# Hybrid pooling and DeltaNet layer: sample's output rows in plain fp32 from refetched raw weights in four column groups, the last z product ahead on VectorE, sample's input rows behind the gate

## The chip, the cores and the metric

The kernel runs on one core of one Trainium2 chip. The metric is the device time of one execution in microseconds; the median over several runs counts. TensorE (PE) multiplies, VectorE (DVE), ScalarE (ACT) and GpSimd (POOL) do elementwise work, and SyncE (SP) issues every DMA from one queue, in program order. PE takes its instructions in program order too, so a wait in front of one instruction holds all behind it.

## What is computed

One decoder layer runs over a prompt of 2048 tokens and over a "sample" of 8 tokens with carried state. The part that the change touches is the output projection of the 8 sample tokens, the products of the SiLU gate, and the input rows of the sample.

```python
h = rms_norm(x, pre_norm_w) * (1.0 + scale[:, None]) + shift[:, None]
proj = h @ w_in                       # u_a, z_a, q, k, v, z_b, b, a
y_a, new_pool = pool_mix(u_a, ...)    # pooling mixer, 4 groups
y_a = y_a * jax.nn.silu(z_a)
o, S = gdn_chunked(q, k, v, g, beta, S0)      # prompt
o, S = gdn_recurrent(q, k, v, g, beta, S0)    # sample: one step per token
o = rms_norm(o, o_norm_w) * silu(z_b)
y = concatenate([y_a, y_b], -1) @ w_out       # [tokens, 1024] @ [1024, 1024]
x = x + gate[:, None] * rms_norm(y, post_norm_w)
```

All of it is in fp32, inputs and outputs.

## The kernel before

The prompt is cut into four blocks of 512 tokens (`it` 0 to 3; the last is `LAST`). Every block runs through 32 weight tiles (`NW`): 0 to 11 are q, k and v, 12 to 23 are z and u, 24 to 31 (`OUT` + m) are quarters of the output projection. Each fp32 weight is split into two rounded parts, hi and lo, and each activation too, so that one fp32 product becomes three fp32r matmuls: hi with hi, hi with lo, lo with hi. Block 0 splits the weights (ScalarE the hi, GpSimd the lo) and SP keeps the pair in DRAM (`kept_w`, 1 MB a tile); the later blocks load the pair into a ring of three slots `wsl`, three tiles ahead: the load of tile n waits until tile n - 3 has been used (`proj`).

`out_tile(it, m)` (L2170 to L2172) does 24 matmuls of 512 columns. Its m from 0 to 3 makes output columns 0 to 511 (`hf` 0), m from 4 to 7 the rest (`hf` 1). The first reads of an accumulator bank wait for VectorE's product of z tile 23, `zmul` (L1370), which frees that bank. Between the tiles of phase two runs a plan of 27 slots with the DeltaNet chain; m = 0 falls in slot 24, m = 1 in slot 26.

In the last block the sample rides along. For the output projection `sample_out(it, m)` (L2236 to L2238) takes the 8 rows `ym2`, split into hi and lo, through the same split weight tile that `out_tile(it, m)` uses: six matmuls with 8 stationary columns and 512 moving ones for each of the eight m, which collect in one bank for each half (`so` 0 and 1). VectorE copies the half to `ys` (`sample_half`, L1401). `sample_state(it, m)` (L2289) multiplies the key rows `krow` (VectorE, L1548), which the new states `ssm` need (L1559, L1563). At the very end `ys` is squared (ScalarE), its root taken (GpSimd), then scaled and added on VectorE (L1849, L1852), before VectorE weighs the last prompt rows (`weigh_rows`, L1286) and adds them to the residual (L1864).

SP's function `load_tile` loads the kept tiles, `xres` brings the residual rows of the prompt (L817), and behind the last of these come sample's inputs and the outputs.

Of the kernel before, what the change touches and what calls it, by code (L numbers as in the profile page):

```python
# [20 lines left out]
F32 = mybir.dt.float32  # L21
# [143 lines left out]
def psum_jobs(it):  # L165
# [25 lines left out]
    for slot, (c, p, sc, q, parts) in enumerate(PLAN):  # L191
# [64 lines left out]
def sample_plan_steps():  # L256
# [4 lines left out]
             "pool": [f"pl{i}" for i in range(9)], "mixed": ["ym0", "ym1", "ym2", "yma", "yh", "yl"],  # L261
# [22 lines left out]
def sample_out_steps():  # L284

    out = []
    for m in range(8):
        out += ["krow0", "krow1"] if m == 0 else [f"krow{m + 1}"] if m < 7 else []
        out += ["ys0"] if m == 4 else []
# [6 lines left out]
    "pe": ["hs"] + [f"{kind}{n}" for kind, n in JOBS[-1] if kind in SAMPLE_JOBS and kind != "so"],  # L296
    "act": ["x_sq"] + sample_act_steps() + ["y_sq"],
    "pool": ["rx0", "rx", "clear", "half", "rk", "rstd", "ry0", "ry"],
    "dve": (["xn", "h0", "h", "hh", "hl"] + ["g_a", "pg0", "g_beta", "g_sp", "g_g", "pg1", "g_d0", "g_d1"] + sample_plan_steps() + sample_out_steps() + ["ys1", "yn", "yr"]),
# [3 lines left out]
def layer_kernel(nc, a):  # L303
    ctx = ExitStack()
    with ctx:
# [83 lines left out]
        lb = over("lb", rp, 0, [P, BS, BS])  # L389
        epar = sb("epar", [P, 2])  # L390
# [10 lines left out]
        ym2 = sb("ym2", [P, 8, 2 * NS], F32R)  # L401
# [286 lines left out]
        def _(sp):  # L688
# [40 lines left out]
            def load_tile(it, t):  # L729
# [3 lines left out]
                if it == LAST and t - WS >= OUT:  # L733
                    sp.wait_ge(*done("pe", f"sp{t - WS}"))
# [4 lines left out]
                sp.dma_start(slot_words(n), kept[t]).then_inc(w_in[n % WS], 16)  # L739

# [22 lines left out]
            def block_of(it, last=False):  # L763
# [8 lines left out]
                for t in range(NW):  # L772
# [377 lines left out]
        def _(dve):  # L1150
# [247 lines left out]
            def sample_half(it, hf):  # L1398

                dve.wait_ge(*done("pe", f"sp{OUT + 4 * hf + 3}"))  # L1400
                nc.vector.tensor_copy(ys[:, hf * BT:(hf + 1) * BT], bank("so", hf)[0:NS, :]).then_inc(*step("dve", f"ys{hf}"))  # L1401

            def sample_slot(it, slot):
# [123 lines left out]
                if slot == SAMPLE_SLOT["mixed"]:  # L1527
# [6 lines left out]
                    after("yma")  # L1534
                    after("ymb")
                    nc.vector.tensor_copy(ym2[:, :, 0:NS], ym[:]).then_inc(*s("yh"))
                    after("yh")
                    nc.vector.tensor_tensor(ym2[:, :, NS:], ym[:], ym2[:, :, 0:NS].bitcast(F32), ALU.subtract).then_inc(*s("yl"))

            def sample_out(it, m):  # L1540
# [54 lines left out]
            def block_of(it, last=False):  # L1595
# [3 lines left out]
                for t in range(NQ):  # L1599
# [25 lines left out]
                    if t == GATES + 2 and it == 0:  # L1625
                        sample_rows()
# [13 lines left out]
                    if t == GATES + 2:  # L1640
# [9 lines left out]
                                                ALU.mult).then_inc(g_g.sem, 1)  # L1650
                    for c in GB_AT.get(t, ()):
# [45 lines left out]
                for slot, (c, p, sc, q, parts) in enumerate(PLAN):  # L1697
# [147 lines left out]
                if last:  # L1845
                    sample_half(it, 1)
# [187 lines left out]
        def _(pe):  # L2034
# [189 lines left out]
            def sample_out(it, m):  # L2224

                hf, kp = divmod(m, 4)
                t = OUT + m
                pe.wait_ge(*weights_in(it, t))
                pe.wait_ge(*done("dve", "yl"))
                if kp == 0:  # L2230
                    bank_free(pe, it, "so", hf)
                for j in range(2):
                    k = 2 * kp + j
# [304 lines left out]
```

## Time and profile before

| | before |
|---|---|
| median of 3 runs | 1060.54 us (1058.96 to 1061.08) |
| profiled execution | 1061.8 us, of which the span from the first to the last instruction is 1060.0 us |
| PE busy | 1019.4 us, 96% of the span |
| VectorE, ScalarE, GpSimd busy | 642.8, 391.2, 218.6 us |
| mean granted TensorE clock | 0.989 |
| HBM read, written | 156.43 MB, 44.81 MB |

Lines "L12" are lines of the kernel before. A row of a timeline gives the start, the duration, the engine, the line and what is written from what; matmuls are pipelined, so a matmul of 512 columns shows some 0.39 us but the next one starts 0.23 us later. In brackets stands how long the engine was idle before, and what ended that. A plain fp32 matmul leaves two records (x2 for one). PEclk is the granted clock, 1.00 for 2.4 GHz and 0.50 for 1.2 GHz.

### The profile page before, as it was taken

Reading aid. Unit: us, or ns where it says so; the run is one execution under the profiler, and the core shown is the slowest. Engines: PE = TensorE matmul, PEld = TensorE weight load, DVE = VectorE, ACT = ScalarE, POOL = GpSimd, SP = SyncE. Lnnn points to the kernel's source line nnn. Section 1 sums busy time; section 2 is a strip of 40 time slices with the busy share of each in tenths; the row PEclk is TensorE's granted clock in tenths of the full one; section 3 lists DMA queues with packets and bytes.
Section 4 is the critical chain, followed back from the end, with each engine's and each line's share of the span. In section 5 each row is a group of like instructions: output and inputs, shape, how many; then the busy total and the mean of one; then the engine's idle time right before and its main releaser. Section 6 shows DMA issues by size and latency. Waiting matters only on the chain.

```text
span 1060.0 us, 16762 instructions
## 1 busy us (share of the span) xinstructions
PE 1019.4 (96%) x6235; PEld 796.3 (75%) x6235; DVE 642.8 (61%) x1344; ACT 391.2 (37%) x773; POOL 218.6 (21%) x222
## 2 busy tenths in 40 slices
PE   4999999999999999999999999999999999999995
PEld 1577677877777788887877788887877788888774
DVE  2468896577355784576356874576255765555644
ACT  4277532433725621323435621414426631121211
POOL 0143545555400102221000102230000100533000
PEclk9999999999999999999999999999999999999998
DMA  8597665373867553244656553254674343322265
GB/s 333 221 354 257 238 252 233 120 257 131 307 214 274 188 190 142 97 160 146 253 200 235 199 198 119 82 192 149 255 293 159 120 159 120 116 77 88 89 241 177
DMA packets 46804, 202.33 MB, mean 191 GB/s; under 512 B 9162, under 2 KB 9930, under 8 KB 29188
## 3 DMA queue, kind: packets, MB, share of 16 engines
q1 hardware_dynamic: 46724, 201.26, 52.0%
q8 instruction: 50, 0.82, 0.3%
q14 instruction: 30, 0.25, 0.1%
HBM read 156.43 MB, written 44.81 MB: 190 GB/s over the span
## 4 chain that ended last, share of the span: by engine, by line
PE 80%; DVE 6%; issue 4%; DMA 3%; ACT 2%; POOL 2%; SPq 1%; DVEq 0%; ACTq 0%; POOLq 0%
PE acc L2133 15%; PE acc L2135 14%; PE acc L2134 14%; PE ring L2183 11%; PE ring L2170 2%; PE acc L2170 2%; PE ring L2171 2%; PE ring L2172 2%; PE acc L2172 2%; PE acc L2171 2%; DMA wraw<-in_w 2%; PE ring L2200 2%; PE ring L2370 1%; DVE cacc L1254 1%; PE ring L2192 1%
## 5 line engine op out<-in xcount | busy, mean ns | idle before, releaser
L2133 PE MATMUL acc<-hhi,wsl 128*128 128x512 f32 x768 | 317.7, 414 | 2.7 <-DVE y L1370 2.6
L2135 PE MATMUL acc<-hhi,wsl 128*128 128x512 f32 x768 | 301.2, 392 | 0.0
L2134 PE MATMUL acc<-hlo,wsl 128*128 128x512 f32 x768 | 300.8, 392 | 0.0
L2133 PEld LDWEIGHTS acc<-hhi,wsl 128*128 128x128 f32 x768 | 145.4, 189 | 41.4 <-issue 10.2
L2135 PEld LDWEIGHTS acc<-hhi,wsl 128*128 128x128 f32 x768 | 144.7, 188 | 31.8
L2134 PEld LDWEIGHTS acc<-hlo,wsl 128*128 128x128 f32 x768 | 145.5, 189 | 27.6 <-issue 2.2
L1254 DVE SCALAR_TENSOR_TENSOR cacc<-raw,cw,cacc 128x512 f32<-128x512 f32 x144 | 113.1, 785 | 66.3 <-ACT cacc L938 59.8
L1905 POOL TENSOR_TENSOR wsl<-wraw,wsl 128x512 fp32r<-128x512 f32 x60 | 84.9, 1429 | 104.2 <-ACT wsl L901 104.2
L934 ACT ACTIVATE raw<-acc 128x512 f32<-128x512 f32 x48 | 28.6, 596 | 123.8 <-PE acc L2135 119.3
L2170 PE MATMUL acc<-wsl,yhi 128*128 128x512 f32 x128 | 51.7, 404 | 5.2 <-DVE y L1370 3.4
L901 ACT ACTIVATE wsl<-wraw 128x512 fp32r<-128x512 f32 x64 | 38.1, 622 | 40.2 <-DMA wraw<-in_w 37.9
L1970 POOL TENSOR_TENSOR on<-on,mhalf 128x4 f32<-128x4 f32 x16 | 23.1, 1446 | 138.8 <-DVE on L1789 138.8
L2170 PE MATMUL ring<-wsl,yhi 128*128 128x512 f32 x128 | 51.1, 400 | 0.4
L2172 PE MATMUL ring<-wsl,yhi 128*128 128x512 f32 x128 | 50.4, 394 | 0.0
L2171 PE MATMUL ring<-wsl,ylo 128*128 128x512 f32 x128 | 50.3, 393 | 0.0
L2172 PE MATMUL acc<-wsl,yhi 128*128 128x512 f32 x128 | 50.0, 391 | 0.0
L2171 PE MATMUL acc<-wsl,ylo 128*128 128x512 f32 x128 | 50.0, 390 | 0.0
L1095 ACT ACTIVATE junk<-ao 128x128 bf16<-128x128 f32 x64 | 19.9, 310 | 74.5 <-DVE ao L1777 72.9
L946 ACT ACTIVATE tmpa<-acc 128x512 f32<-128x512 f32 x32 | 19.1, 597 | 69.5 <-PE acc L2135 69.1
L997 ACT ACTIVATE cq<-cacc 128x512 f32<-128x512 f32 x48 | 30.2, 629 | 31.0 <-DVE cacc L1254 30.8
L1339 DVE TENSOR_TENSOR xt<-xt,stmp 128x126 f32<-128x126 f32 (+22 forms) x124 | 37.7, 304 | 4.3
L1336 DVE TENSOR_TENSOR stmp<-lb,xt 128x126 f32<-128x126 f32 (+22 forms) x124 | 36.6, 295 | 3.6
(323 smaller groups left out, 1668.0 us busy)
## 6 DMA issues: line engine op xcount, KB each, us to landing
wsl<-kept_w SPq DMA_DIRECT2D x96, 1024.0 KB, 4.8
kept_w<-wsl SPq DMA_DIRECT2D x32, 1024.0 KB, 6.4
wraw<-in_w SPq DMA_DIRECT2D x64, 256.0 KB, 4.3
xb<-in_x SPq DMA_DIRECT2D x16, 512.0 KB, 5.7
wada<-in_w_ada SPq DMA_DIRECT2D x8, 1024.0 KB, 11.5
xres<-in_x SPq DMA_DIRECT2D x16, 512.0 KB, 5.7
out_y<-ytok SPq DMA_DIRECT2D x16, 512.0 KB, 8.0
xtr<-in_xt SPq DMA_DIRECT2D x12, 512.0 KB, 6.6
```

The costliest lines, as they stand in the source:

```text
L901: nc.scalar.activation(wsl[:, t % WS, 0, e * (KT // 2):(e + 1) * (KT // 2)], wraw[:, n % WR], ACT.Copy).then_inc(w_hi, 1)
L1254: nc.vector.scalar_tensor_tensor(out=cacc[:, t % 2], in0=r[:, j:j + BT], scalar=cw[:, t, j:j + 1], in1=cacc[:, t % 2], op0=ALU.mult, op1=A ...
L1336: nc.vector.tensor_tensor(t, lb[:, m, 0:m].unsqueeze(2).to_broadcast([P, m, n]), xt[:, m, m // 2:].unsqueeze(1).to_broadcast([P, m, n]), A ...
L1339: nc.vector.tensor_tensor(xt[:, 0:m, m // 2:], xt[:, 0:m, m // 2:], t, ALU.subtract).then_inc(sub_f.sem, 1)
L1905: nc.gpsimd.tensor_tensor(wsl[:, t % WS, 1, ks], wraw[:, n % WR], wsl[:, t % WS, 0, ks].bitcast(F32), ALU.subtract).then_inc(w_lo, 1)
L2133: nc.tensor.matmul(acc[t % 2][:], w[:, 0, k], hi[:, k], start=(k == 0), stop=False)
L2134: nc.tensor.matmul(acc[t % 2][:], w[:, 0, k], lo[:, k], start=False, stop=False)
L2135: last = nc.tensor.matmul(acc[t % 2][:], w[:, 1, k], hi[:, k], start=False, stop=(k == KT - 1))
L2170: nc.tensor.matmul(o, yhi[:, k, cols], w_hi_k, start=(k == 0), stop=False)
L2171: nc.tensor.matmul(o, ylo[:, k, cols], w_hi_k, start=False, stop=False)
L2172: last = nc.tensor.matmul(o, yhi[:, k, cols], w_lo_k, start=False, stop=(k == KT - 1))
L2183: last = nc.tensor.matmul(bank(kind, i)[rows, h * n:(h + 1) * n], left(h), right(h), start=True, stop=True)
```

## The change

Sample's output rows are made from raw fp32 weights instead of the split ones. `sample_out(it, hf)` is called twice: half 0 where m = 0 and 1 stood, half 1 in front of `sample_state(it, 5)`. Each call is eight plain fp32 matmuls with `ym` as stationary operand, k going round four column groups of 32, so four partial sums land in partitions 0, 32, 64 and 96 of one bank. VectorE adds them up (one copy and three adds for each half). The raw weights, 512 KB for each m, are fetched a second time by SP into four buffers `wout0` to `wout3` laid over other tiles. Beside it, `zmul` of tile 23 goes to the front of slot 23's work in all four blocks, and in block 0 `sample_rows` (the sample's input rows) goes behind the gate's softplus chain. The split of `ym` (two small VectorE operations) goes, and so do SP's waits for the sample's matmuls ahead of the last five weight tiles.

```diff
@@ SP
             def load_tile(it, t):
                 n = it * NW + t
                 sp.wait_ge(*proj(*divmod(n - WS, NW)))
-                if it == LAST and t - WS >= OUT:
-                    sp.wait_ge(*done("pe", f"sp{t - WS}"))
...
+            def sample_out_weights(m):
+                sp.dma_start(wout[m % 4][:].rearrange("p j c -> p (j c)"), a["w"][OUT + m].rearrange("p k c -> p (k c)")
+                             ).then_inc(raw_in[WR - 1], 16)
...   (in the loop over t, behind load_tile(it, t + WS) and xres)
+                    if last and t == OUT - 2:
+                        sp.wait_ge(*conv(it, NQ - 1))
+                        sp.wait_ge(*hist_out(it, NQ - 1))
+                        sample_out_weights(0)
+                        sp.wait_ge(*pooled_f(it, NG - 1))
+                        sp.wait_ge(*u_out(it, NG - 1))
+                        sample_out_weights(1)
+                        sample_out_weights(2)
+                    if last and t == OUT - 1:
+                        sp.wait_ge(*done("pe", f"sc{OUT // 4 - 1}"))
+                        sample_out_weights(3)
+                    if last and t == OUT + 4:
+                        sp.wait_ge(*done("pe", "so0"))
+                        for m in range(4, 8):
+                            sample_out_weights(m)
@@ DVE, sample_half
-                dve.wait_ge(*done("pe", f"sp{OUT + 4 * hf + 3}"))
-                nc.vector.tensor_copy(ys[:, hf * BT:(hf + 1) * BT], bank("so", hf)[0:NS, :]).then_inc(*step("dve", f"ys{hf}"))
+                cols = slice(hf * BT, (hf + 1) * BT)
+                dve.wait_ge(*done("pe", f"so{hf}"))
+                nc.vector.tensor_copy(ys[:, cols], bank("so", hf)[0:NS, :]).then_inc(*step("dve", f"ys{hf}a"))
+                for g, so_far, to in ((1, "a", "b"), (2, "b", "c"), (3, "c", "")):
+                    dve.wait_ge(*done("dve", f"ys{hf}{so_far}"))
+                    nc.vector.tensor_tensor(ys[:, cols], ys[:, cols], bank("so", hf)[g * BS:g * BS + NS, :], ALU.add
+                                            ).then_inc(*step("dve", f"ys{hf}{to}"))
...   (the second half: was behind the loop over m, now at m == 7, ahead of L1559)
@@ DVE, slots
             def gated(it, t):
-                zmul(it, t)
+                if t < OUT - 1:
+                    zmul(it, t)
...   (slot 23, ahead of its job "ot")
+                    if slot == LAST_PART:
+                        zmul(it, OUT - 1)
@@ PE, sample_out(it, hf) in place of sample_out(it, m)
-                for j in range(2):
-                    k = 2 * kp + j
...
-                    nc.tensor.matmul(o, ym2[:, k, 0:NS], w_hi_k, start=(k == 0), stop=False)
-                    nc.tensor.matmul(o, ym2[:, k, NS:], w_hi_k, start=False, stop=False)
-                    last = nc.tensor.matmul(o, ym2[:, k, 0:NS], w_lo_k, start=False, stop=(k == KT - 1))
+                bank_free(pe, it, "so", hf)
+                pe.wait_ge(*done("dve", "yma"))
+                pe.wait_ge(raw_in[WR - 1], 16 * (len(range(WR - 1, 2 * NW, WR)) + 4 * (hf + 1)))
+                for k in range(KT):
+                    kp, j = divmod(k, 2)
+                    g = k % NBK
+                    last = nc.tensor.matmul(bank("so", hf)[g * BS:g * BS + NS, :], ym[:, k], wout[kp][:, j], start=(k < NBK),
+                                            stop=(k >= KT - NBK))
...   (behind slot 26, the loop over m)
                 for m in range(8):
-                    if last and m >= 2:
-                        sample_out(it, m)
+                    if last and m == 5:
+                        sample_out(it, 1)
```

Three places show what moves. On PE, in the last block at m = 5 (`wsl` and `yhi` are the prompt's weights and rows, `wout` the raw weights, `ym` the sample's rows), before:

```order
L2171 MATMUL ring5<-wsl_68,ylo_53 128x512
L2172 MATMUL ring5<-wsl_68,yhi_52 128x512
L2236 MATMUL ring3<-wsl_68,ym2 8x512 [waits sample_dve,w_in1]
L2237 MATMUL ring3<-wsl_68,ym2 8x512
L2238 MATMUL ring3<-wsl_68,ym2 8x512
L2236 MATMUL ring3<-wsl_68,ym2 8x512
L2237 MATMUL ring3<-wsl_68,ym2 8x512
L2238 MATMUL ring3<-wsl_68,ym2 8x512
L2289 MATMUL ring1<-drow_114,krow_117 128x128 [waits sample_dve]
```

and of the change at the same place:

```order
L2191 MATMUL ring5<-wsl_68,ylo_53 128x512
L2192 MATMUL ring5<-wsl_68,yhi_52 128x512
L2252 MATMUL ring3<-wout0_86,ym_110 8x512 [waits raw_in2,sample_dve,ya_f]
L2252 MATMUL ring3<-wout0_86,ym_110 8x512
L2252 MATMUL ring3<-wout1_87,ym_110 8x512 x2
L2252 MATMUL ring3<-wout2_88,ym_110 8x512 x2
L2252 MATMUL ring3<-wout3_89,ym_110 8x512 x2
L2304 MATMUL ring1<-drow_118,krow_121 128x128 [waits sample_dve]
```

The six split matmuls ahead of the state's give way to all eight of half 1, which wait for the DMA semaphore `raw_in2`. Nothing of the sample's output stands at m = 2, 3, 4, 6 and 7 any more.

On SP, in the last block, from the residual load ahead of the last weight tile to the first output (`xs` and `gr8` are the sample's residual and gate rows), before:

```order
L817 DMA xres_59<-in_x 128x1024
L739 DMA wsl_68<-kept_w 128x2048 [waits sample_pe,proj]
L817 DMA xres_59<-in_x 128x1024
L820 DMA xs_118<-in_xs 8x1024 [waits proj]
L822 DMA gr8_119<-gate_rows 8x1024 [waits gate_out]
```

and of the change:

```order
L818 DMA xres_59<-in_x 128x1024
L735 DMA wsl_68<-kept_w 128x2048 [waits proj]
L818 DMA xres_59<-in_x 128x1024
L739 DMA wout0_86<-in_w 128x1024 [waits sample_pe]
L739 DMA wout1_87<-in_w 128x1024
L739 DMA wout2_88<-in_w 128x1024
L739 DMA wout3_89<-in_w 128x1024
L836 DMA xs_122<-in_xs 8x1024 [waits proj]
```

The four raw tiles of half 1 stand behind the load of tile 31 (L735), whose wait for `proj` is for tile 28, the tile of m = 4, and behind the last residual load.

On VectorE, in slots 23 and 24 of block 2 (`xtr` is the next block's input), before:

```order
L1829 TENSOR_TENSOR xtr<-xtr,rxb 128x512
L1804 SCALAR_TENSOR_TENSOR y_60<-ring,vec,y_60 128x4x128 [waits z_f,job_ot]
L1271 TENSOR_TENSOR ylo<-y_60,yhi 128x512 [waits yhi_f] x2
L1829 TENSOR_TENSOR xtr<-xtr,rxb 128x512
L1370 SCALAR_TENSOR_TENSOR y_60<-tmpa,acc 128x512 [waits job_w,tanh_f]
L1592 SCALAR_TENSOR_TENSOR y_60<-ring,vec,y_60 128x512 [waits z_f,job_pool]
```

and of the change:

```order
L1850 TENSOR_TENSOR xtr<-xtr,rxb 128x512
L1386 SCALAR_TENSOR_TENSOR y_60<-tmpa,acc 128x512 [waits job_w,tanh_f]
L1825 SCALAR_TENSOR_TENSOR y_60<-ring,vec,y_60 128x4x128 [waits z_f,job_ot]
L1287 TENSOR_TENSOR ylo<-y_60,yhi 128x512 [waits yhi_f] x2
L1850 TENSOR_TENSOR xtr<-xtr,rxb 128x512
L1611 SCALAR_TENSOR_TENSOR y_60<-ring,vec,y_60 128x512 [waits z_f,job_pool]
```

`zmul` (L1370, now L1386) moves ahead of the gated head outputs, the two ylo splits and one xtr product.

## Rows read from the trace of the kernel before

**Rows 1.** The page, busy time, share and instructions of PE first.
```profile
PE 1019.4 (96%) x6235; PEld 796.3 (75%) x6235; DVE 642.8 (61%) x1344; ACT 391.2 (37%) x773; POOL 218.6 (21%) x222
```
**Rows 2.** Waits, 60 to 80 us: total, times, longest, in us.
```profile
DVE gsp L1643 <- ACT gl L1036: 0.9, 1, 0.9
```
**Rows 3.** Timeline of PE, block 0.
```profile
248.78 0.47 PE L2170 MATMUL acc<-wsl,yhi 128*128 128x512 f32 x1
...
251.62 0.50 PE L2170 MATMUL acc<-wsl,yhi 128*128 128x512 f32 x1 [1.91 <-DVE y L1370]
...
258.28 0.39 PE L2170 MATMUL acc<-wsl,yhi 128*128 128x512 f32 x1
```
**Rows 4.** Timeline of VectorE, block 0.
```profile
250.89 0.68 DVE L1370 SCALAR_TENSOR_TENSOR y<-tmpa,acc 128x512 f32<-128x512 f32 x1
...
255.31 1.29 DVE L1271 TENSOR_TENSOR ylo<-y,yhi 128x512 fp32r<-128x512 f32 x2 [1.70 <-ACT yhi L962]
```
**Rows 5.** Windows: stretch, length, busy times, then granted clock, DMA share, GB/s.
```profile
71.60:74.90 3.30, 3.30 (x15) 2.49 (x8) 3.06 (x7) 3.24 (x5) 1.47 (x2) 0.50 0.75 256
252.30:255.60 3.30, 3.30 (x9) 2.48 (x8) 1.60 (x4) 2.45 (x10) 0.00 (x0) 0.53 0.69 292
723.60:726.90 3.30, 3.26 (x14) 2.72 (x15) 1.94 (x3) 1.74 (x9) 0.00 (x0) 1.00 0.00 0
```
**Rows 6.** Timeline of PE, block 2.
```profile
723.64 0.51 PE L2170 MATMUL acc<-wsl,yhi 128*128 128x512 f32 x1 [0.76 <-DVE y L1370]
```
**Rows 7.** Timeline of PE, last block, m = 3.
```profile
1011.64 0.40 PE L2236 MATMUL ring<-wsl,ym 128*8 128x512 f32 x1
...
1013.02 0.56 PE L2289 MATMUL ring<-drow,krow 96*128 96x128 f32 x4
```
**Rows 8.** Timeline of PE, last block, m = 0 to 2.
```profile
1003.04 1.23 PE L2289 MATMUL ring<-drow,krow 96*128 96x128 f32 x8 [0.15 <-DVE krow L1548]
...
1005.63 0.63 PE L2289 MATMUL ring<-drow,krow 96*128 96x128 f32 x4
```
**Rows 9.** Timeline of VectorE, last block.
```profile
1002.21 1.28 DVE L1548 TENSOR_TENSOR krow<-drow,own 96x512 fp32r<-96x512 f32 x2
...
1004.80 0.68 DVE L1548 TENSOR_TENSOR krow<-drow,own 96x512 fp32r<-96x512 f32 x1
```
**Rows 10.** Timeline of PE: plain fp32 in three, then in four column groups.
```profile
125.78 5.34 PE L2079 MATMUL ring<-wada,cpad 128*32 128x512 f32 x32
...
898.54 1.94 PE L2265 MATMUL ring<-ssm,km 128*16 128x128 f32 x64
```
**Rows 11.** Timeline of SP's queue, last block.
```profile
975.64 9.15 SPq L739 DMA_DIRECT2D wsl<-kept_w  x2
...
1011.83 0.32 SPq L739 DMA_DIRECT2D wsl<-kept_w  x1
1012.20 0.43 SPq L817 DMA_DIRECT2D xres<-in_x  x1
```
**Rows 12.** DMA issues, 1011.5 to 1013 us: KB each, us to landing.
```profile
wsl<-kept_w SPq DMA_DIRECT2D x1, 1024.0 KB, 4.8
xres<-in_x SPq DMA_DIRECT2D x1, 512.0 KB, 5.7
```
**Rows 13.** Windows, with DMA's GB/s last.
```profile
1013.00:1017.00 4.00, 4.00 (x21) 3.34 (x20) 0.69 (x1) 0.00 (x0) 0.00 (x0) 1.00 0.87 353
20.00:30.00 10.00, 8.11 (x38) 2.77 (x37) 5.34 (x15) 5.14 (x8) 0.72 (x2) 0.86 1.03 410
```
**Rows 14.** Timeline of VectorE, end of the last block.
```profile
1042.90 0.69 DVE L1563 TENSOR_TENSOR ssm<-ssm,ring 128x512 f32<-128x512 f32 x1 [6.03 <-PE ring L2289]
...
1048.74 1.27 DVE L1286 TENSOR_TENSOR ytok<-acc,gpw 128x512 f32<-128x512 f32 x2
...
1051.79 4.87 DVE L1864 SCALAR_TENSOR_TENSOR ytok<-ytok,ry,xres 128x1024 f32<-128x1024 f32 x4 [0.52 <-POOL ry L2016]
```
**Rows 15.** Timeline of ScalarE, end of the last block.
```profile
1048.79 0.60 ACT L972 ACTIVATE junk<-ring 128x512 bf16<-128x512 f32 x1
```

More of the change, by code:

```diff
@@ L224, in psum_jobs @@
         jobs.append(("xf", m))
-        if m == 4:
+        if m == 5:
             jobs.append(("so", 1))
-        if m >= 2:
-            jobs.append(("sp", OUT + m))
         jobs.append(("sop", m))
@@ L260, in sample_plan_steps @@
              "mean": ["own0", "own1", "dh", "dk", "drow", "ms0", "ms1", "ms2"], "gate": ["zs", "on", "ymb"],
-             "pool": [f"pl{i}" for i in range(9)], "mixed": ["ym0", "ym1", "ym2", "yma", "yh", "yl"],
+             "pool": [f"pl{i}" for i in range(9)], "mixed": ["ym0", "ym1", "ym2", "yma"],
              "joined": ["pg5a", "pg5"]}
@@ L288, in sample_out_steps @@
         out += ["krow0", "krow1"] if m == 0 else [f"krow{m + 1}"] if m < 7 else []
-        out += ["ys0"] if m == 4 else []
+        out += [f"ys{m // 7}{g}" for g in "abc"] + [f"ys{m // 7}"] if m in (4, 7) else []
         out += [f"se{m}", f"sn{m}"]
@@ L295 @@
 SAMPLE_STEPS = {
-    "pe": ["hs"] + [f"{kind}{n}" for kind, n in JOBS[-1] if kind in SAMPLE_JOBS and kind != "so"],
+    "pe": ["hs"] + [f"{kind}{n}" for kind, n in JOBS[-1] if kind in SAMPLE_JOBS],
     "act": ["x_sq"] + sample_act_steps() + ["y_sq"],
     "pool": ["rx0", "rx", "clear", "half", "rk", "rstd", "ry0", "ry"],
-    "dve": (["xn", "h0", "h", "hh", "hl"] + ["g_a", "pg0", "g_beta", "g_sp", "g_g", "pg1", "g_d0", "g_d1"] + sample_plan_steps() + sample_out_steps() + ["ys1", "yn", "yr"]),
+    "dve": (["xn", "h0", "h", "hh", "hl"] + ["g_a", "pg0", "g_beta", "g_sp", "g_g", "pg1", "g_d0", "g_d1"] + sample_plan_steps() + sample_out_steps() + ["yn", "yr"]),
 }
@@ L389, in layer_kernel @@
         lb = over("lb", rp, 0, [P, BS, BS])
+        wout = [over(f"wout{n}", base, 0, [P, 2, BT]) for n, base in enumerate((rr_, ru, rv_, rw))]
         epar = sb("epar", [P, 2])
@@ L1558, in sample_out @@
                     sample_half(it, 0)
+                if m == 7:
+                    sample_half(it, 1)
                 nc.vector.tensor_tensor(ssm[:, m], ssm[:, m], gvb[:, m, 1].unsqueeze(2).to_broadcast([P, H, P]),
@@ L1624, in block_of @@
                         gate_sums(it)
-                    if t == GATES + 2 and it == 0:
-                        sample_rows()
                     if t == GATES + 1:
@@ L1650, in block_of @@
                                                 ALU.mult).then_inc(g_g.sem, 1)
+                    if t == GATES + 2 and it == 0:
+                        sample_rows()
                     for c in GB_AT.get(t, ()):
@@ L2222, in sample_join, with sample_out @@
                 last.then_inc(*step("pe", f"sc{g}"))
[L2224 to L2231, printed above, removed]
-                for j in range(2):
-                    k = 2 * kp + j
-                    w_hi_k, w_lo_k = (wsl[:, slot(it, t), e].rearrange("p k c -> p (k c)")[:, j * BT:(j + 1) * BT] for e in range(2))
-                    o = bank("so", hf)[0:NS, :]
-                    nc.tensor.matmul(o, ym2[:, k, 0:NS], w_hi_k, start=(k == 0), stop=False)
-                    nc.tensor.matmul(o, ym2[:, k, NS:], w_hi_k, start=False, stop=False)
-                    last = nc.tensor.matmul(o, ym2[:, k, 0:NS], w_lo_k, start=False, stop=(k == KT - 1))
-                last.then_inc(*step("pe", f"sp{t}"))
+            def sample_out(it, hf):
+                bank_free(pe, it, "so", hf)
[6 more added lines that the diff above has]
+                                            stop=(k >= KT - NBK))
+                last.then_inc(*step("pe", f"so{hf}"))
             def sample_slot(it, slot):
```

10 lines of the change are left out of this document (1 added, 9 removed).

## The prediction

> **What bounds the kernel now.** I read the page first: PE is busy for 1019.4 us, 96% of the span [rows 1]. Only work that leaves PE's queue, or a wait in it, can move the time; VectorE at 61% matters where PE waits for it. So next I took PE's waits, then the timeline at each place that the change touches, then SP's queue and the rate of DMA, because the change adds 4 MB of loads.
>
> Three places matter.
>
> First, out_tile 0. In block 0, PE starts it at 248.78, stops after three matmuls, and goes on at 251.62, after 1.91 us of idleness that VectorE's L1370 ends [rows 3]. That product had been free to run since ScalarE's tanh, and stood behind the head outputs, two ylo splits and xtr; it starts at 250.89 [rows 4]. A second price follows: from 252.3 to 255.6 the granted clock is 0.53, almost all of it at the lower level of 1.2 GHz [rows 5]. Blocks 1 and 2 wait 0.76 us at the same place, at the full clock ([rows 6] is block 2; block 1 reads alike). The last block doesn't wait there.
>
> Second, the sample's output. From 1011.64 to 1013.02, 1.38 us, PE does its six matmuls of one m [rows 7], with no idleness at all.
>
> Third, the end. VectorE does the sample's last rows first and weighs the prompt's rows only from 1048.74 on, though ScalarE's squares of the last tile begin at 1048.79 and the first three tiles' come before that [rows 14, 15].
>
> **The change, part by part.**
>
> *zmul ahead.* In block 0 PE no longer stops for L1370. Out_tile 1 started at 258.28 [rows 3]; without the wait and the slow clock tile 0 takes 24 x 0.23 = 5.5 us, so it ends at 254.3. Then ylo 2 is late next: its split begins at 255.31, behind ScalarE [rows 4]; with one VectorE product of 0.6 us gone from in front of it, it is done at about 255.3. Tile 1 starts there: 258.3 - 255.3 = 3.0, taken as 2.9. Blocks 1 and 2: 0.76 each, as ylo 2 is ready in time there by the same shift. Last block: none. Sum -4.4 us. Bounds: -2.5 (the clock falls in block 0 all the same) to -5.
>
> *sample_rows behind the gate.* Nothing. Before gsp (L1643) VectorE was idle for 0.9 us until ScalarE's logarithm came [rows 2]: the four small operations in front of it weren't late. Behind it they take 1.0 us, in which PE computes the gate's sums anyway. If that cover is short, it costs 0.3 us.
>
> *m = 0 to 2 of the sample.* These matmuls are mostly hidden already. State 0 starts at 1003.04 because VectorE's krow came then [rows 8], and state 2 at 1005.63 just after the krow product of 1004.80 [rows 8, 9]; VectorE's chain there is unchanged. PE has less to do between, and waits about 1.4 us ahead of 1003.04 and 1.5 us ahead of 1005.63. Gain 0, and out_tile 2 starts when it did.
>
> *m = 3 to 7.* Five times 1.38 us goes: -6.9. Out_tile 4 also needs ytok of tile 0 to 3; ScalarE squares these tiles as they end and VectorE weighs them, at 0.78 us a tile, and by that pace each bank is free about 0.5 us before it is needed once the 1.38 us in front is gone, so I add nothing.
>
> *The fp32 matmuls.* Sixteen of 512 columns with 8 stationary columns. In the trace, 16 of 512 columns in three groups take 5.34 us, and 32 of 128 columns in four groups take 1.94 with the last one's tail [rows 10], 1.7 from start to start. Eight of 512 in four groups are the same columns as that: 1.75 us for half 1. Half 0 falls into the wait for krow. +1.75. Bounds: three-group rate 2.65, and 1.7. VectorE's three adds on 8 x 512 each cost as much as its copy, 0.67 us; they stand behind states with over a microsecond of idleness, and at m = 7 nearly 4 us lie between the last two states. Nothing.
>
> *The refetch, half 0.* Its first three tiles can leave when tile 25's load leaves, at 975.64, the fourth behind the one at 984 [rows 11]. Each such bunch lands within 8 us, before 999.9. SP's new waits (convolution, pooling, join) are all past by then and hold no load up. Nothing.
>
> *The refetch, half 1.* This is the step that decides. The SP rows put these four loads behind load_tile(31), which waits for tile 28, that is out_tile 4; and the PE rows put half 1 directly behind out_tile 4. So PE stops when SP is first allowed to issue. What must land then: 1 MB for tile 31, 0.5 MB residual, 2 MB raw. The same first 1.5 MB were issued at 1011.83 and 1012.20 and the second landed 5.7 us after its issue, 6.1 after the first's [rows 11, 12]. The further 2.1 million bytes go at 410 GB/s, the rate where many loads queue [rows 13]: 5.1 us. With 0.2 us from tile to issue that is 11.4 us of wait. Bounds: 0.2 us and all 3.67 million bytes at 410 GB/s, with no latency at all, 9.2; the further ones at 353 [rows 13], 12.2. Behind the waiting matmul stand states 5 to 7 and three output tiles, everything that ends the kernel; behind SP's loads stand only outputs.
>
> The Trainium skill (DMA: Bandwidth & Descriptors, Anatomy of one DMA) fits a load from GpSimd's path as 2.0 us plus the bytes at 436 GB/s. For these bytes it would give 10.4 us, and a sum smaller by 1.0; SP's queue here is another path, and no row shows so long a bunch at the end of the kernel.
>
> *The clock.* After idle stretches the clock falls: 1.91 us idle in block 0 was followed by 3.3 us at the lower level, and so was a stretch around 70 us with 1.28 us of idleness and small matmuls after it [rows 3, 5]. Twice 3.3 us at half the speed costs 1.6 us each. Behind the wait of 11 us I count one: +1.6. The second place is m = 0 to 2, where 2.9 of 4.5 us now are idle: +1.6 as well. Bounds for each: 0 and 3.3.
>
> The Trainium skill (TensorE: Matmul & The Clock Gate, HAM oscillation) describes just this: a DMA wait between bursts of matmuls that makes the next burst start cold. It speaks against half 1's place; the trace agrees as far as its shorter gaps go.
>
> *The end.* ys of half 1 is ready early, so its root no longer holds VectorE. Before, L1563 of state 7 came at 1042.90 and the weighing began at 1048.74. Now the two operations on 8 x 1024 rows follow the state directly and end some 2.6 us sooner; weighing then goes at ScalarE's pace, whose last square runs from 1048.79 to 1049.4 [rows 14, 15]. The root of the prompt's rows can follow at 1049.6 and take 1.0 us, so L1864 starts near 1050.8 in place of 1051.79. -1.0. Bounds 0 and -1.2.
>
> **Sum.** -4.4 - 6.9 + 1.75 + 11.4 + 1.6 + 1.6 - 1.0 = +4.05 us. The profiled execution took 1061.8 us with a span of 1060.0, and would show a span near 1064.0. The runs' median, 1060.54, lies 1.3 below the profiled time; the same difference on it gives 1064.6.
>
> **The rivals.** A measurement of this kernel tells 0.2%, 2.1 us, from no change, so the limits are 1058.4 and 1062.7.
>
> *Wait long, clock kinder (no change), 0.22.* The two small gaps at m = 0 to 2 are cut by states and may not bring the clock down, and the wait may be 10.3 us, half way to its lower bound. For it: behind block 2's 0.76 us of idleness the clock stayed at 1.00 [rows 5, 6]. That is 4.05 - 1.6 - 1.1 = +1.35: 1061.9.
>
> *The loads are there in time (faster), 0.09.* If half 1's weights cost PE nothing, the sum is -4.4 - 6.9 + 1.75 - 1.0 = -10.55, or 1050.0, with the m = 0 to 2 clock 1051.6. It decides when wait and clock together stay below 8.4 us. Against it stands the order of both queues; a transfer would have to take less than 6 us for 3.67 million bytes, over 600 GB/s, against 410 in [rows 13].
>
> *The other bound (slower still), 0.11.* The 410 GB/s need not hold while small writes come in behind, and the clock may stay down twice as long after so long a gap: +1.2 + 1.6 on the sum, and up to 2 us less from zmul in block 0 as the split weights aren't ready sooner: 1067.5 to 1069.
>
> *The change doesn't do what it says.* If the four groups ran one after another, half 1 would take 8 x 0.85 = 6.8 us, +5: 1069.6. [rows 10] speak against it; 0.02.
>
> My forecast, the wait that costs more than all gains: 0.56, with a range of 1062.7 to 1067.
>
> **How the numbers follow.** Slower holds the forecast and the last two rivals, 0.69; the same 0.22; faster 0.09. The range from 1061.0 to 1068.5 leaves out the faster case and about half of the slowest.
>
> **What would show it.** PE idle some 11 us ahead of the eight matmuls of half 1, released by a DMA of wout; the granted clock at 0.5 behind it and perhaps around 1006; 1.7 us from the first to the last start of those matmuls; no idleness for zmul at out_tile 0 in any block; L1563 to L2289 periods of 5.9 us instead of 7.3 in the last block; about 1.0 us less between the last matmul and the end. Wrong would make me: half 1's weights landed in under 6 us, a ytok wait that eats the 1.38 us at out_tile 4, or block 0's gain lost again to the split weights.

## The result and the profile after

| | before | after |
|---|---|---|
| median | 1060.6 us (14 runs, 1056.2 to 1062.2) | 1066.6 us (14 runs, 1064.0 to 1070.9) |
| ratio of after to before | | 1.0064, 95% interval 1.0050 to 1.0077 |
| profiled execution, span | 1061.8, 1060.0 us | 1066.9, 1065.1 us |
| mean granted TensorE clock | 0.989 | 0.984 |
| HBM read | 156.43 MB | 160.63 MB |

The change makes the kernel 0.6% slower, 6.0 us between the medians. The prediction was 1064.6 us with a range of 1061.0 to 1068.5, and it gave "slower" a chance of 0.69.

Line numbers have moved: L2190 to L2192 are `out_tile`, L2252 is the sample's output in fp32, L2304 `sample_state`, L1386 `zmul`, L1564 the key rows, L735 `load_tile`, L739 the raw weights.

The page, which answers to [rows 1], first:

```profile
PE 1013.4 (95%) x6219; PEld 794.4 (75%) x6219; DVE 649.7 (61%) x1348; ACT 391.2 (37%) x773; POOL 218.6 (21%) x222
```

PE is busy for 6.0 us less and yet the kernel takes longer. So its time went into waiting. The waits of PE over the whole span (total, times, longest):

```profile
PE ring L2252 <- DMA wout<-in_w: 12.9, 1, 12.9
...
PE ring L2304 <- DVE krow L1564: 2.5, 2, 1.4
...
PE ring L2190 <- DVE y L1611: 1.3, 1, 1.3
PE ring L2338 <- DVE gg L1665: 1.1, 1, 1.1
```

The first row is the answer in one line. Its place is in the timeline of PE in the last block, from the last head turn to the last state (these rows answer to [rows 7, 8]):

```profile
993.45 0.60 PE L2220 MATMUL ring<-ident,ao 128*128 128x128 f32 x4
993.98 1.90 PE L2252 MATMUL ring<-wout,ym 128*8 128x512 f32 x16
996.98 1.24 PE L2304 MATMUL ring<-drow,krow 96*128 96x128 f32 x8 [1.09 <-DVE krow L1564]
999.57 0.90 PE L2304 MATMUL ring<-drow,krow 96*128 96x128 f32 x4 [1.36 <-DVE krow L1564]
1007.16 0.56 PE L2304 MATMUL ring<-drow,krow 96*128 96x128 f32 x4
1013.10 0.56 PE L2304 MATMUL ring<-drow,krow 96*128 96x128 f32 x4
1032.05 3.60 PE L2252 MATMUL ring<-wout,ym 128*8 128x512 f32 x16 [12.86 <-DMA wout<-in_w]
1035.58 1.12 PE L2304 MATMUL ring<-drow,krow 96*128 96x128 f32 x4
1042.43 0.56 PE L2304 MATMUL ring<-drow,krow 96*128 96x128 f32 x4
1048.36 0.56 PE L2304 MATMUL ring<-drow,krow 96*128 96x128 f32 x4
```

The same marks before, the last head turn and states 4 and 7 (states 0 to 3 are in [rows 7, 8]):

```profile
999.51 0.60 PE L2200 MATMUL ring<-ident,ao 128*128 128x128 f32 x4
...
1020.35 0.56 PE L2289 MATMUL ring<-drow,krow 96*128 96x128 f32 x4
...
1042.31 0.56 PE L2289 MATMUL ring<-drow,krow 96*128 96x128 f32 x4
```

The starts of states 0 to 7 (L2304, before L2289) are the marks to read; states 0 and 1 share one row. State 3 to state 4 takes 5.94 us here and took 7.33 before: each m is 1.39 us shorter. State 4 to state 5 takes 22.48 us: 5.93 for an output tile and a state, 12.86 of wait, 3.53 for half 1, and the rest is the wait's own, because a row counts idleness from a modelled end. Half 1's row shows 3.60 where half 0's shows 1.90. The factor of two is the clock. Windows of the changed kernel (granted clock, DMA share and GB/s last):

```profile
1000.00:1002.00 2.00, 2.00 (x7) 1.70 (x7) 1.90 (x4) 0.00 (x0) 0.00 (x0) 0.50 0.00 0
1002.00:1004.00 2.00, 2.00 (x8) 1.55 (x7) 1.90 (x4) 0.00 (x0) 0.00 (x0) 0.71 0.00 0
...
1024.00:1026.00 2.00, 0.00 (x0) 0.00 (x0) 0.00 (x0) 0.00 (x0) 0.00 (x0) 0.50 1.04 420
1026.00:1028.00 2.00, 0.00 (x0) 0.00 (x0) 0.00 (x0) 0.00 (x0) 0.00 (x0) 0.50 1.04 401
1028.00:1030.00 2.00, 0.00 (x0) 0.00 (x0) 0.00 (x0) 0.00 (x0) 0.00 (x0) 0.50 1.01 281
1030.00:1032.00 2.00, 0.00 (x0) 0.00 (x0) 0.00 (x0) 0.00 (x0) 0.00 (x0) 0.50 1.01 303
1032.00:1036.00 4.00, 3.95 (x18) 0.90 (x19) 0.00 (x0) 0.00 (x0) 0.00 (x0) 0.50 0.95 231
1036.00:1038.00 2.00, 2.00 (x9) 1.77 (x9) 1.27 (x3) 0.00 (x0) 0.00 (x0) 0.67 0.97 366
```

The clock is at its lower level (0.50, 1.2 GHz) in two places: from 1000 to about 1003 us, behind the two short gaps, and from within the long wait to about 1037. The rate of DMA falls from 400 and more to about 290 GB/s at 1028, while the share of busy engines stays at 1.0. SP's queue shows what came in behind the four loads (start, time to issue):

```profile
1019.22 0.32 SPq L735 DMA_DIRECT2D wsl<-kept_w  x1
1019.58 0.43 SPq L818 DMA_DIRECT2D xres<-in_x  x1
1020.06 2.13 SPq L739 DMA_DIRECT2D wout<-in_w  x4
...
1022.96 0.37 SPq L843 DMA_DIRECT2D out_o_ssm<-st  x1
...
1024.84 0.49 SPq L852 DMA_DIRECT2D out_o_sconv<-pj  x1
```

The whole account, from marks of before to the same marks of after in the two profiled executions. To part wait, clock and work behind state 2, it takes the full-clock times from the run with earlier loads below, which is the same kernel without the wait: 5.97 us from state 2 to state 3, 6.02 from state 4 to half 1's start, 1.84 from there to state 5, 6.04 from state 5 to state 6.

| stretch | predicted | measured |
|---|---|---|
| start of the kernel to the head turn at 246.32 (before), 245.09 (after) | 0 | -1.2 |
| from there to the last head turn, 999.51 and 993.45 (`zmul`) | -4.4 | -4.8 |
| last head turn to state 2, 6.12 in both | 0 | 0 |
| m = 3 to 7, six matmuls less each | -6.9 | -7.0 |
| half 1's fp32 matmuls at full clock, with 0.2 around them | +1.75 | +2.0 |
| half 1's wait | +11.4 | +12.9 |
| lower clock around 1000 us | +1.6 | +1.6 |
| lower clock behind the wait | +1.6 | +2.5 |
| last state to the end, 17.69 and 16.74 | -1.0 | -0.95 |
| span | +4.05 | +5.1 |

### The profile page after: what moved, and what is told of

Its sections match the earlier page's. It is cut to its first block, busy times and chain, and to the rows that moved or that the text cites. A ratio compares the mean times of both kernels' runs of the same rounds, so it can differ in the third digit from the quotient of the medians.

```text
span 1065.1 us, 16732 instructions
## 1 busy us (share of the span) xinstructions
PE 1013.4 (95%) x6219; PEld 794.4 (75%) x6219; DVE 649.7 (61%) x1348; ACT 391.2 (37%) x773; POOL 218.6 (21%) x222
## 3 DMA queue, kind: packets, MB, share of 16 engines
HBM read 160.63 MB, written 44.81 MB: 193 GB/s over the span
## 4 chain that ended last, share of the span: by engine, by line
PE 82%; DVE 5%; DMA 4%; issue 3%; ACT 2%; POOL 2%; SPq 1%; DVEq 0%; ACTq 0%; POOLq 0%
PE acc L2153 15%; PE acc L2155 14%; PE acc L2154 14%; PE ring L2203 11%; PE ring L2190 3%; PE acc L2190 3%; PE ring L2191 2%; PE ring L2192 2%; PE acc L2191 2%; PE acc L2192 2%; DMA wraw<-in_w 2%; PE ring L2220 2%; PE ring L2385 1%; PE ring L2212 1%; DVE cacc L1270 1%
## 5 line engine op out<-in xcount | busy, mean ns | idle before, releaser
L2190 PE MATMUL acc<-wsl,yhi 128*128 128x512 f32 x128 | 51.8, 405 | 1.6 <-POOL wsl L1925 1.5
L2190 PE MATMUL ring<-wsl,yhi 128*128 128x512 f32 x128 | 50.7, 396 | 1.7 <-DVE y L1611 1.3
L2192 PE MATMUL acc<-wsl,yhi 128*128 128x512 f32 x128 | 50.4, 394 | 0.0
L2192 PE MATMUL ring<-wsl,yhi 128*128 128x512 f32 x128 | 49.9, 390 | 0.0
L1302 DVE TENSOR_TENSOR ytok<-acc,gpw 128x512 f32<-128x512 f32 x16 | 11.1, 692 | 46.3 <-ACT junk L988 45.6
```

Of the source, the lines that this page charges most:

```text
L2190: nc.tensor.matmul(o, yhi[:, k, cols], w_hi_k, start=(k == 0), stop=False)
L2192: last = nc.tensor.matmul(o, yhi[:, k, cols], w_lo_k, start=False, stop=(k == KT - 1))
```

## The experiments

Three theories stood at the start. *Place*: the change is good work at a bad place; the wait and the clock behind it, then reckoned at 15.6 us, hide a gain. *Cost*: the 4 MB fetched again and the plain fp32 matmuls cost by themselves. *Writes*: the small outputs behind the loads stretch the wait. Each ratio below is to the kernel before, run on the same chip.

### Half 1's loads earlier

```diff
-                    if last and t == OUT + 4:
+                    if last and t == OUT + 1:
                         sp.wait_ge(*done("pe", "so0"))
```

> The change with the four loads of half 1 issued at tile OUT + 1, behind half 0's last read of the buffers, in place of OUT + 4; all else as it is. Theory (the place of the loads decides): they leave near 996 us and land some 10 us later, long before half 1's matmuls; the wait of 12.9 us and the 2.7 us of slow clock behind it go, so 1066.6 - 15.6 = 1051.0 us (1049.5 to 1053). Rival (the 4 MB fetched again and the plain fp32 matmuls cost by themselves): the wait turns up elsewhere, at the weight tiles 28 to 30 whose loads now queue behind 2 MB, and the time stays above 1058 us.

Measured: 1051.28 us against 1059.24, ratio 0.9919 (0.9895 to 0.9944). The timeline of PE has no wait in front of half 1, which now stands at full clock:

```profile
1012.95 0.56 PE L2304 MATMUL ring<-drow,krow 96*128 96x128 f32 x4
1018.97 1.90 PE L2252 MATMUL ring<-wout,ym 128*8 128x512 f32 x16
1020.81 0.66 PE L2304 MATMUL ring<-drow,krow 96*128 96x128 f32 x4
```

State 4 to state 5 takes 7.86 us in place of 22.48, and state 4 to state 7 takes 19.83 in place of 35.26, 15.4 less. SP issued the four loads at 997.41, and their bytes went by at 399 to 416 GB/s without anyone waiting (window 998 to 1004 us). The same bytes, the same matmuls, one number in SP's loop: *place* holds and *cost* falls.

### The product of z tile 23 alone

```diff
 (the kernel before)
-                zmul(it, t)
+                if t < OUT - 1:
+                    zmul(it, t)
...
+                    if slot == LAST_PART:
+                        zmul(it, OUT - 1)
```

> The kernel before with only the product of z tile 23 put ahead in slot 23. Theory (it takes away three waits of PE and one slow stretch of the clock): -2.6 us in block 0 and -1.0 in blocks 1 and 2 each, 1060.6 - 4.6 = 1056.0 us (1055 to 1057). Rival (a wait only moves to the next VectorE product in the queue): -1 to -2 us, 1059 us.

Measured: 1054.92 us against 1059.24, ratio 0.9951 (0.9934 to 0.9969). From the turn near 246 us to the last head turn this kernel takes 748.50 us; before takes 753.19 and after 748.36. So the whole -4.7 comes with this part alone. And the reverse, the product put back in the changed kernel:

> The change with the product of z tile 23 left where it stood before. Theory (its gain is independent of the rest): the waits of 1.9 and twice 0.8 us at out_tile 0 come back, 1066.6 + 4.7 = 1071.3 us. Rival (part of that gain was owed to something else in the change): under 1070 us.

Measured: 1069.82 us, ratio 1.0088 (1.0063 to 1.0114), 3 us above the change's own 1066.6, where 4.7 was expected. The median lies just on the rival's side of 1070; the interval reaches the expected 1071.3, so the times alone don't decide. The stretch between the marks takes 752.98 us, 4.6 more than after, so the trace carries the theory. Block 0's wait is back (timeline of PE in this kernel), and the clock is at 0.50 in the window from 252 to 254 us behind it:

```profile
251.17 0.50 PE L2187 MATMUL acc<-wsl,yhi 128*128 128x512 f32 x1 [1.91 <-DVE y L1386]
```

### No writes beside the loads

```diff
+            sp.wait_ge(*done("pe", "so1"))
             sp.wait_ge(*s_f(LAST, NC - 1))
             sp.dma_start(a["o_ssm"], st[:]).then_inc(out_sem, 16)
```

> The change with SP holding the first outputs of the last block back until half 1's matmuls are done, so no write runs beside the four loads. Theory (small writes take rate from the loads ahead of them): the wait before half 1 falls from 12.9 to 11.4 us, the reads keep some 400 GB/s to the end of the bunch, 1065.1 us. Rival (the bunch's reads are slow by themselves at their end): wait 12.9 us, 1066.6 us. Second rival (writes held back end later than the prompt's rows): over 1067 us.

Measured: 1065.66 us, ratio 1.0048 (1.0030 to 1.0067), not told apart from the change by these intervals. The trace does: the wait is 12.14 us in place of 12.86 (12.73 and 12.76 in the two kernels with the `zmul` or the key rows moved, which have the writes), and the windows that had 281 and 303 GB/s have 418 and a short rest:

```profile
1028.00:1030.00 2.00, 0.00 (x0) 0.00 (x0) 0.00 (x0) 0.00 (x0) 0.00 (x0) 0.50 1.02 418
1030.00:1032.00 2.00, 0.00 (x0) 0.01 (x1) 0.00 (x0) 0.00 (x0) 0.00 (x0) 0.50 0.31 121
```

So *writes* is real and small: 0.6 to 0.7 us of the 1.5 by which I had the wait too short. The rest is in the bunch itself, and finer windows show where:

```profile
1021.50:1022.00 0.50, 0.00 (x0) 0.00 (x0) 0.14 (x1) 0.00 (x0) 0.00 (x0) 0.92 0.39 147
1022.00:1030.50 8.50, 0.00 (x0) 0.00 (x0) 0.00 (x0) 0.00 (x0) 0.00 (x0) 0.50 1.01 411
1030.50:1031.00 0.50, 0.00 (x0) 0.00 (x0) 0.00 (x0) 0.00 (x0) 0.00 (x0) 0.50 0.24 74
1031.00:1031.50 0.50, 0.00 (x0) 0.00 (x0) 0.00 (x0) 0.00 (x0) 0.00 (x0) 0.50 0.00 0
```

SP issues the first load at 1019.92. Until 1020.5 nothing moves, then 131 to 147 GB/s until 1022, then 411 GB/s, and from about 1030.7 on nothing again until half 1 starts at 1032.02. So the rate was as predicted. Of the 12.1 us from the first issue to that start, some 3.2 are the two ends (12.1 less 3.67 million bytes at 411 GB/s), where the prediction's 6.1 us for the first two loads hold 2.3 (6.1 less 1.57 million bytes at 410). Why the end without any bytes lasts 1.3 us, no run here tells.

### Half 1 later, loads unchanged

```diff
-                    if last and m == 5:
+                    if last and m == 7:
                         sample_out(it, 1)
```

> The change with half 1's matmuls ahead of state 7 in place of state 5; the loads stay at OUT + 4. Theory (only the time between issue and use counts, not the bytes or where they are fetched): PE does two more output tiles in between, 11.9 us at full clock, and then waits for 12.9 - 11.9 = 1.0 us; with no slow clock behind it the time is 1066.6 - 11.9 - 2.7 = 1052.0 us (1051 to 1054.5, the upper end if VectorE's four operations on ys hold the last state's sum). Rival (reads that run beside output tiles and small writes are slowed or slow the weight tiles): over 1056 us.

Measured: 1053.08 us against 1059.29, ratio 0.9943 (0.9929 to 0.9956). Here the writes do run beside the loads, and PE waits for only 0.57 us:

```profile
1030.22 1.90 PE L2252 MATMUL ring<-wout,ym 128*8 128x512 f32 x16 [0.57 <-DMA wout<-in_w]
```

The wait can be taken away at either end, by an earlier issue or a later use. The later use is 1.8 us dearer than the earlier issue by the medians, but the two ratios' intervals overlap. The traces show where it can come from: the last state to the end takes 18.84 us here and 16.72 with the earlier issue. In this kernel's trace VectorE does half 1's copy and three adds, 1032.19 to 1034.95, in front of the last state's sum; the two operations on 8 x 1024 rows start at 1037.13, 5.07 us after the last state, where they start 1.20 us after it in the change. The expectation's upper part had named this.

### PE kept busy through the wait

```diff
+                if hf:
+                    for n in range(54):
+                        nc.tensor.matmul(bank("so", 1)[:], yhi[:, n % KT, 0:P], yhi[:, n % KT], start=True, stop=True)
                 pe.wait_ge(raw_in[WR - 1], ...)
```

> The change with 54 further matmuls of 128 x 512 into half 1's own bank (its first real matmuls clear it) ahead of the wait for the four loads; their products are used nowhere. They take 54 x 0.217 = 11.7 us of the 12.9 us that PE waits. Theory (the clock falls because PE idles, and costs 2.7 us on top of the wait): the wait shrinks to some 1.2 us, the granted clock stays at 1.00, and 1066.6 - 2.7 = 1063.9 us. Rival (the slow stretch behind the wait has nothing to do with PE's idleness): 1066.6 us. Second rival (the filling delays the real matmuls): 1067 us or more.

Measured: 1064.56 us, ratio 1.0050 (1.0036 to 1.0063), 2.0 us under the change by the medians and 1.5 by the ratios, whose intervals overlap; the trace decides. The filling took 12.40 us, where 11.7 was expected, so next to nothing of the wait was left, and half 1 ran at full clock:

```profile
1020.74 12.40 PE L2250 MATMUL ring<-yhi 128*128 128x512 f32 x54
1033.26 1.90 PE L2255 MATMUL ring<-wout,ym 128*8 128x512 f32 x16
1035.09 0.66 PE L2307 MATMUL ring<-drow,krow 96*128 96x128 f32 x4
1041.09 0.56 PE L2307 MATMUL ring<-drow,krow 96*128 96x128 f32 x4
```

From state 4 to state 6 (1014.80 to 1041.09) it takes 26.29 us; in the change, 1013.10 to 1042.43, 29.33. Of these 3.0 us, 0.5 lie ahead of half 1 (state 4 to half 1's start takes 18.46 here and 18.95 in the change). From half 1's start to state 6 it is 7.83 against 10.38, so 2.5 us of the change's loss is the clock's and not the wait's. This separates the two.

The 2.5 is one execution's. The kernel that holds the outputs back has nearly the same wait, and its clock was up again sooner:

```profile
1032.02 3.60 PE L2253 MATMUL ring<-wout,ym 128*8 128x512 f32 x16 [12.14 <-DMA wout<-in_w]
1035.55 0.66 PE L2305 MATMUL ring<-drow,krow 96*128 96x128 f32 x4
1041.57 0.56 PE L2305 MATMUL ring<-drow,krow 96*128 96x128 f32 x4
```

That is 9.55 us from half 1's start to state 6. It was 9.42 behind the wait of 12.73 in the kernel with `zmul` put back and 9.29 behind the 12.76 in the one with the key rows moved. Against 7.83 the slow clock behind the wait cost 1.7, 1.6 and 1.5 us there.

### One column group

```diff
 (on top of the earlier loads)
-                    g = k % NBK
-                    last = nc.tensor.matmul(bank("so", hf)[g * BS:g * BS + NS, :], ym[:, k], wout[kp][:, j], start=(k < NBK),
-                                            stop=(k >= KT - NBK))
+                    last = nc.tensor.matmul(bank("so", hf)[0:NS, :], ym[:, k], wout[kp][:, j], start=(k == 0),
+                                            stop=(k == KT - 1))
...   (and sample_half without its three adds)
```

> early_loads with all sixteen fp32 matmuls in one column group, so they run one after another, and VectorE's three adds per half left out. Theory (four groups run at once): eight take 8 x 0.85 = 6.8 us in place of 1.8; +5.0 us for half 1, and for half 0 +5.0 less the 2.45 us that PE waits for the key rows, so 1051.3 + 7.5 = 1058.8 us. Rival (the groups overlap by half only): +4 us, 1055 us. Second rival (VectorE's adds cost as much as the groups save): 1051.3 us.

Measured: 1059.02 us, ratio 0.9998 (0.9983 to 1.0012): 7.7 us more than with four groups by the medians, 8.4 by the ratios, so both rivals fall. Half 0 costs 3.5 us more up to state 2 (9.62 from the last head turn, against 6.13), where 2.5 was expected: it covers only 1.4 of the 2.45 us that PE waits for the key rows. Half 1 in this kernel, 7.0 us to the next start in place of 1.84:

```profile
1023.31 7.03 PE L2247 MATMUL ring<-wout,ym 128*8 128x512 f32 x16
1030.28 0.66 PE L2299 MATMUL ring<-drow,krow 96*128 96x128 f32 x4
```

Four groups run 3.8 times as fast as one. Without them the fp32 path would have given back all that the rest gains.

### The sample's input rows alone

```diff
 (the kernel before, in VectorE's loop over t: this call moves)
-                    if t == GATES + 2 and it == 0:
-                        sample_rows()
...
                         nc.vector.tensor_tensor(gg[:], gsp[:]...)
+                    if t == GATES + 2 and it == 0:
+                        sample_rows()
```

> The kernel before with only the sample's input rows moved behind the gate's softplus and product. Theory (VectorE waits there for ScalarE's logarithm in any case): 0, within the 1.5 us that the start of the kernel varies; PE's wait for gg falls by 0.2 us at most. Rival (the four small operations now stand in front of the decay products, which PE waits for): +1 us.

Measured: 1060.2 us against 1059.29, ratio 1.0008 (0.9993 to 1.0024): no difference that can be measured. PE's wait for gg is 1.2 us, 1.3 before; VectorE's own wait for the logarithm grows from 0.9 to 1.9 us, so what moved away had filled it.

### The key rows earlier

```diff
 (VectorE, slot 26, ahead of the last head output; key_rows(0) to (2) leave sample_out)
+                    if last and sc == NC - 1 and q == 3:
+                        dve.wait_ge(*proj(it, OUT - 1))
+                        dve.wait_ge(*done("dve", "drow"))
+                        for r in range(3):
+                            key_rows(r)
```

> As early_loads, and the first three key row products on VectorE go ahead of the last head output in slot 26, into 3.3 us in which VectorE was idle. Theory (PE's waits of 1.09 and 1.36 us before states 1 and 2, and the slow clock from 1000 to 1003 us, come from VectorE's order): both waits and most of the 1.66 us of slow clock go, less 0.6 us for state 2 that then waits for its bank: 1051.0 - 3.5 = 1047.5 us (1046.5 to 1049). Rival (states wait for the bank that the state before last frees, so the idleness only changes its name): under 1 us less than early_loads.

Measured: 1048.17 us against 1059.24, ratio 0.9886 (0.9866 to 0.9906), the fastest version here: 1.1% under the kernel before and 3.1 us under the earlier loads alone. The two ratios' intervals just touch; in the traces the last head turn to state 3 takes 10.29 us, against 12.10 and 13.70 in the two executions of the earlier loads (the second with the slow clock). The same edit on the change itself:

> The change with the first three key row products ahead of the last head output on VectorE; the loads of half 1 stay at OUT + 4. Theory (the key rows' order costs 2.45 us of waits and, in this kernel, 1.66 us of slow clock from 1000 to 1003 us): 1066.6 - 2.4 + 0.8 (state 2 then waits for its bank) - 1.7 = 1063.3 us; half 1's wait stays at 12.9 us. Rival (what PE saves there it only waits longer for half 1's loads): impossible if the loads' issue moves along with out_tile 4; then 1066.6 us.

Measured: 1062.52 us against 1059.18, ratio 1.0026 (1.0009 to 1.0043). States 0 to 3 in its timeline:

```profile
997.32 1.11 PE L2306 MATMUL ring<-drow,krow 96*128 96x128 f32 x8
999.19 0.66 PE L2306 MATMUL ring<-drow,krow 96*128 96x128 f32 x4 [0.76 <-DVE ssm L1578]
1005.24 0.56 PE L2306 MATMUL ring<-drow,krow 96*128 96x128 f32 x4
```

State 2 to 3 takes 6.05 us in place of 7.59, so the clock stayed up, and of 2.45 us of waits 0.76 is left, with a new releaser: the bank. Half 1's wait stays at 12.76, as it must, since its loads are issued behind the same output tile.

### The clock near 1000 us, in a second execution

> The same kernel as early_loads, for a second profile. In its first one the granted clock stayed at 1.00 behind the two gaps of 1.09 and 1.36 us before states 1 and 2, where four other kernels with the same gaps fell to 0.50. Theory (it depends on when the gaps fall, from execution to execution): the clock may fall here, and states 2 and 3 are then 7.6 us apart in place of 6.0. Rival (the loads that run beside the gaps in this kernel keep it up): 1.00 again, 6.0 us.

Measured: one execution, 1050.67 us. The gaps of 1.09 and 1.36 us are the same, the loads run beside them at 416 GB/s, and this time the clock fell:

```profile
1000.00:1002.00 2.00, 2.00 (x6) 1.61 (x5) 1.90 (x5) 0.00 (x0) 0.00 (x0) 0.50 1.01 416
```

States 2 and 3 are 7.58 us apart. The rival falls: the loads don't keep the clock up.

## Why the prediction was right, point by point

**Half 1's wait.** The mechanism was as told: SP's queue puts the loads behind tile 28's use, PE's queue puts their reader there too, and the wait takes what the 3.67 million bytes need. The size was 1.5 us too small. The rate of 410 GB/s held; writes behind the loads cost 0.6 to 0.7 us, and the two ends of the longer bunch, where few or no bytes move, last 3.2 us where the term's 6.1 us for the first two loads had 2.3. The bound of 12.2 that I gave was exceeded by 0.7.

By the fit in the Trainium skill (DMA: Bandwidth & Descriptors, Anatomy of one DMA) an estimate for these bytes is 10.4 us; measured are 12.1 without and 12.9 with the writes. The measurement decides, and the page gives the fit for a single DMA on GpSimd's path, not for a bunch in SP's queue.

**The clock.** Both places came as told. The one at 1000 us cost 1.6 us as predicted. The one behind the long wait cost 2.5, not 1.6: 1.7 in half 1 itself and 0.8 up to state 6. I had taken 3.3 us at the lower level from [rows 5]; here it was some 5 us, from 1032 to about 1037. That is this profiled execution: behind three other waits of 12.1 to 12.8 us it cost 1.5 to 1.7, so 1.6 was a fair size and the 0.9 above it is within what one execution can add. The run that filled the wait shows the price apart from the wait. The Trainium skill (TensorE: Matmul & The Clock Gate, HAM oscillation) has the burst behind a DMA wait start cold; the trace agrees, with a granted clock of 0.50 from half 1's first matmul on.

**zmul ahead.** -4.7 to -4.8 measured for -4.4, and alone it moves the median by -4.3. That the sum fits so well is partly luck, for its parts were off both ways. Block 0 gives -2.4, not -2.9, because out_tile 0 waits for another product there, L1611 for 1.28 us, and not for ylo 2, which I had named as next. It stands behind two ylo splits that take 2.75 us here:

```profile
246.39 2.75 DVE L1287 TENSOR_TENSOR ylo<-y,yhi 128x512 fp32r<-128x512 f32 x2
249.06 0.68 DVE L1850 TENSOR_TENSOR xtr<-xtr,rxb 128x512 f32<-128x512 f32 x1
249.67 0.74 DVE L1611 SCALAR_TENSOR_TENSOR y<-ring,vec,y 128x512 f32<-128x512 f32 x1
```

The clock did not fall behind that wait. Blocks 1 and 2 give -1.0 each, not -0.76: the idleness in a row is counted from a modelled end, and the step from start to start is the price to take. The last 0.3 to 0.4 us of the stretch lie between these places (from the head turn at 263.73 to the one at 485.83 it took 222.10 us before, 221.82 in the change), and no run ties them to `zmul`.

**m = 3 to 7, fp32, end, sample rows.** -7.0 for -6.9, +2.0 for +1.75, -0.95 for -1.0, and 0 for 0. At the end VectorE does what was told: L1869 at 1049.56 directly behind the last state's sum, and the final L1864 of before, now L1884, at 1056.85, 8.49 us behind the last state where it was 9.48.

**The sum.** The medians moved by 6.0 us, 2.0 more than the 4.05 predicted; the two profiles differ by only 5.1, because the start of the kernel happened to be 1.2 shorter in the changed one. Nearly all of the 2.0 is the wait's 1.5 and the clock's 0.9 of this execution.

**The rivals.** The loads in time are what the earlier issue made of this kernel: 1051.3 measured, 1050.0 to 1051.6 given for it. The kinder clock did not come. The "other bound" named both terms that came out too short: writes beside the loads cost 0.6 to 0.7 us, and the clock stayed down for some 5 us; block 0's gain was not lost again to the split weights, as it had feared. One group was priced at +5 for half 1 and came at +5.1.

What stays open: why the bunch has such ends, and when a gap of a microsecond brings the clock down (last section).

## What to carry to other kernels

A load's cost is set by the distance between where its queue may issue it and where it is read: find both places in program order, and if the same instruction stands before each, the whole transfer is exposed, however well it is hidden elsewhere. Look for the latest *real* release of the buffer (here half 0's read, 24 us earlier) and issue there; here that one number turned +0.6% into -0.8%. A long wait has a second price in the clock behind it, and a change with several parts should be priced part by part, since -11 us of good edits were invisible behind 17 us of waiting and slow clock.

## What the runs showed of the hardware

- Behind a wait of 12.86 us the clock stayed at its lower level for about 5 us of dense matmuls, a price of 2.5 us; behind waits of 12.14, 12.73 and 12.76 us in three other kernels it rose after some 3 to 3.6 us, a price of 1.5 to 1.7 us, no more than the 3.3 us behind a gap of 1.9 us [rows 5].
- A bunch of six loads, 3.67 million bytes, in SP's queue moved at 411 GB/s for 8.5 us, but 12.1 us passed from the first issue to the matmul that waited for it: 0.6 without any bytes, 1.5 at 131 to 147 GB/s, and 1.3 at the end without any.
- Plain fp32 matmuls of 8 stationary and 512 moving columns: eight in four column groups took 1.84 us to the next start, eight in one group 6.97.
- Two gaps of 1.09 and 1.36 us, with small matmuls between, brought the clock down in six of the seven profiled executions that had them, and not in the first one of the earlier loads. Where it fell, states 2 and 3 came 7.6 us apart four times and 8.7 us twice, for 6.0 at full clock: a price of 1.6 or 2.7 us. A gap of 0.76 alone (twice) and of 1.02 alone (once) did not. Nor does a long gap decide by itself: the 1.91 us at out_tile 0 in block 0 brought the clock down in the kernel before and in the one without `zmul` ahead, but with only the sample's input rows moved it stayed at 1.00 behind the same gap. Same gaps, two answers: a forecast can give such a gap only a chance.
- Small output writes issued behind large reads took the rate of all bytes together from about 410 to 281 and 303 GB/s though the DMA engines' busy share stayed at 1.01; with the writes held back it kept 418.
- The start of the kernel varies by itself: one of its first small matmuls (at 45.41 us before) came between 43.19 and 45.69 us over the thirteen profiled executions. The -1.2 us at the start of the changed kernel's profile lies inside that, so it is no effect of the change that could be shown. Later in block 0 a stretch that takes 42.9 us before (163.57 to 206.44) took 46.9 and 47.1 us in two kernels that touch nothing there (the sample's input rows alone, and the earlier loads with the key rows); the granted clock from 163.5 to 173.8 us was 0.53 and 0.52 in them and 1.00 before.
